# Loads, splits and small products at the head of a two-layer hybrid encoder kernel, in another order

## The chip, the core and the metric

The kernel runs on one core of a Trainium2 chip. The metric is the device time of one execution in microseconds (us), as the median of several runs; lower is better. The engines of the core are named PE (TensorE, the products), ACT (ScalarE), DVE (VectorE), POOL (GpSimd) and SP (SyncE, which here only issues transfers). ACT issues transfers too, on a queue of its own.

## What is computed

One inference step of a two-layer encoder trunk. 512 prompt tokens and 32 sample tokens, 544 in all, of width 1024, go through two layers. Only the beginning of a layer matters here: an RMS norm, a combined projection, and the low-rank gate of the gated linear attention (GLA).

```python
def rmsnorm(x, w):
    xf = x.astype(jnp.float32)
    y = xf * lax.rsqrt(jnp.mean(xf * xf, axis=-1, keepdims=True) + EPS)
    return (y * w.astype(jnp.float32)).astype(x.dtype)
...
    proj = (hn @ w_in_l).astype(jnp.float32)
...
    log_f = jax.nn.log_sigmoid(low @ w_a2_l.astype(jnp.float32) + b_a_l.astype(jnp.float32)) / GLA_TAU
```

`low` is 16 columns of `proj`. Retention, GLA, band attention, the output projection and a relu-squared MLP with 4096 hidden features follow in each layer, and a last RMS norm at the end.

## The kernel before

Activations stand with features on the partitions: `h` is 8 tiles (kc = 0 to 7) of 128 features by 544 tokens, held in SBUF throughout. Weights come as units of 128 by 1024 (512 KB): a unit is the 8 blocks of 128 by 128 that give 128 output features. A layer has 100 units: 28 of the input projection, 8 of the output projection, 64 of the MLP. Four buffers `raw[0..3]` take them in turn.

Products run in a fast float format of fewer bits, so each operand is split in two: `whi` (a rounded copy, made by ACT in `split`) and `wlo` (the rest, made by DVE in `rest`), and likewise `xhi` (`xhi_tile`, ACT, which also multiplies by the norm weights in the table `sm`) and `xlo` (`xlo_tile`, DVE). There are two buffers each of `whi` and `wlo`. A product block is three matmuls, whi by xhi, whi by xlo and wlo by xhi, over two halves of 272 tokens: 6 matmuls for each unit and kc, 48 for a unit (`products`).

The factor 1/rms is not put in ahead of the projection but afterwards, on the results. For it ACT squares the tiles (`squares`, into `nt[0]` and `nt[1]` in turn), DVE adds them up in `ssum` (`add_square`), and PE sums over the partitions with a matrix of ones (stage "rms", whole-array fp32 matmuls, 2 of them). DVE reads that out of PSUM into `ssum` (L908), makes `wlo` of unit 2, and then does a Newton step that ends in `rstd`. The low-rank product is stage "low": 16 small matmuls, each on a quarter of the array's columns, of `low_sb` (the low-rank weights, times the norm weights by `scale_low` on DVE) and `h`; it needs neither xhi nor xlo. Its result is multiplied by `rstd` and goes into stage "z".

What sets the order: each engine's program is written out by hand, in a function for each engine, and semaphores join them. PE does units 0 and 1 first; in layer 0 kc by kc, both units side by side, as the x tiles come in. Then, for each unit n from 2 on and each half of its tokens, it does the small stages listed in the table `PE_STEPS` under (n, half), and then the products. The tables `DVE_STEPS` and `ACT_STEPS` are copies of it with changes; both layers use them. Unit 2's accumulators share PSUM banks with the result of "rms", so `begin(2)` on PE waits for the semaphore `ms_ready`, which L908 raises, besides `w_lo`, which the third `rest` raises. (The program counts these over both layers.)

At the head of layer 0 the transfers are: on SP's queue x0, x1, x2, raw[1], x3 to x7, `low_sb`, `a2_sb`, raw[2], raw[3] and eight tables; on ACT's queue raw[0] and then the norm table `sm` (28 KB). Ahead of all products PE does 16 warm-up matmuls on ones.

Of the kernel before, what the change touches and what calls it, by code (L numbers as in the profile page):

```python
# [8 lines left out]
D = 1024  # L9
KC = D // P  # L10
# [15 lines left out]
UNITS = N_IN + N_OUT + GROUPS * N_MLP  # L26
PW = 2 * T
NEG = -1e30
YP = 2
WARM = 16  # L30
M0 = 4
# [5 lines left out]
ALU, ACT = mybir.AluOpType, mybir.ActivationFunctionType  # L37
# [6 lines left out]
GLA, RET = 0, 1  # L44
TOK = [(GLA, "v"), (GLA, "k"), (RET, "k"), (RET, "v")]
PE_STEPS = {
    (2, 0): [("rms",), ("low",)],
    (3, 0): [("z", 0)], (3, 1): [("z", 1)],
    (5, 0): [("diag", GLA)],
    (5, 1): [("level", 0)], (6, 0): [("level", 1)], (6, 1): [("level", 2)],  # L50
# [76 lines left out]
def f32(ap):  # L127
    return ap.bitcast(F32)
# [19 lines left out]
def hybrid_encoder(nc, x, wu, w_low, a2, small, bias, bias_s, st_ret, st_gla, ck, cv,  # L148
# [3 lines left out]
    with ctx:  # L152
# [95 lines left out]
        def sem(name):  # L248
            if name not in sems:
                sems[name] = ctx.enter_context(nc.semaphore(name))  # L250
            return sems[name]


        tables_in, sm_in, const_set, half_done, last_added = (
            sem(n) for n in ("tables_in", "sm_in", "const_set", "half_done", "last_added"))
        x_in = [sem(f"x_in{kc}") for kc in range(KC)]
        y_sums, y_mean, y_log, y_guess, y_col, y_wide, y_copied, y_scaled, y_dve, y_pool, y_out = (
            sem(n) for n in ("y_sums", "y_mean", "y_log", "y_guess", "y_col", "y_wide", "y_copied", "y_scaled",
# [21 lines left out]
        with nc.Block() as block:  # L280
            @block.sync
            def _(sp):
                for kc in range(KC):
                    sp.dma_start(h[:, kc, :], x[kc, :, :]).then_inc(x_in[kc], 16)
                    if kc == 2:
                        sp.dma_start(raw[1][:, :], wu[1, :, :]).then_inc(sems["w_in1"], 16)
                sp.dma_start(low_sb[:, :, :], w_low[0, :, :, :]).then_inc(sems["small_in"], 16)
                sp.dma_start(a2_sb[:, :], a2[0, :, :]).then_inc(sems["small_in"], 16)
                for n in range(2, RAW):
# [154 lines left out]
            def _(act):  # L444
# [4 lines left out]
                    ins.then_inc(sems["act_link"], 1)  # L449
                    act.wait_ge(sems["act_link"], links[0])  # L450

                act.dma_start(raw[0][:, :], wu[0, :, :]).then_inc(sems["w_in0"], 16)
                act.dma_start(sm[:, :], small).then_inc(sm_in, 16)

                for layer in range(L):
                    nth = counter(layer)
# [2 lines left out]
                    def split(n):  # L459

                        unit = layer * UNITS + n
                        if unit >= L * UNITS:
                            return
                        act.wait_ge(sems[f"w_in{n % RAW}"], 16 * (unit // RAW + 1))
                        if unit >= SPL:
                            act.wait_ge(sems["unit_done"], unit - SPL + 1)
                        nc.scalar.activation(whi[n % SPL][:, :], raw[n % RAW][:, :], ACT.Copy).then_inc(sems["w_hi"], 1)  # L467
# [5 lines left out]
                    def squares(kc, at_layer, cols=slice(0, T)):  # L473
                        if kc >= 2:
                            act.wait_ge(sems["ss_ready"], at_layer * KC + kc - 1)
                        nc.scalar.activation(nt[kc % 2][:, cols], h[:, kc, cols], ACT.Square).then_inc(sems["squared"], 1)

                    if layer == 0:
                        split(0)
                        act.wait_ge(sm_in, 16)  # L480
                        for kc in range(KC):
                            act.wait_ge(x_in[kc], 16)
                            xhi_tile(kc, 0)
                            if kc == 0:
                                split(1)
                            squares(kc, 0)
                    split(2)

# [260 lines left out]
            def _(dve):  # L749
# [7 lines left out]
                for layer in range(L):  # L757
# [12 lines left out]
                    def xlo_tile(kc, w, count):  # L770
                        dve.wait_ge(sems["x_hi"], nth("x_hi", count))
                        nc.vector.scalar_tensor_tensor(xlo[:, kc, :], h[:, kc, :], sm[:, w + kc:w + kc + 1],
                                                       f32(xhi[:, kc, :]), ALU.mult, ALU.subtract) \
                            .then_inc(sems["x_lo"], 1)
# [23 lines left out]

                    if layer == 0:
                        dve.wait_ge(sm_in, 16)  # L800
                        xlo_tile(0, 0, 1)
                        rest(0)
                        rest(1)
                        add_square(0, 0)
                        for kc in range(1, KC):
                            xlo_tile(kc, 0, kc + 1)
                            add_square(kc, 0)
                        scale_low(0)

                    def unit_out(n):  # L810

# [469 lines left out]
            def _(pe):  # L1281
# [6 lines left out]
                for layer in range(L):  # L1288
# [290 lines left out]

                    all_kc = tuple(range(KC))  # L1580
                    if layer == 0:
                        for kc in range(KC):
                            pe.wait_ge(sems["x_lo"], kc + 1)
                            for n in range(2):
                                if kc == 0:
                                    begin(n)
                                products(n, (xhi, xlo), (kc,), kc == 0, kc == KC - 1)
                    else:
                        pe.wait_ge(sems["x_lo"], nth("x_lo", KC - 1))
                        for n in range(2):  # L1590
                            begin(n)
                            products(n, (xhi, xlo), all_kc[:-1], last=False)
                        pe.wait_ge(sems["x_lo"], nth("x_lo", KC))
                        for n in range(2):
                            products(n, (xhi, xlo), all_kc[-1:], first=False)
# [187 lines left out]
```

## Time and profile before

| | |
|---|---|
| median of 3 runs | 1430.77 us (1430.03 to 1432.64) |
| the profiled execution's own time | 1430.05 us |
| its span, first to last instruction | 1428.2 us |
| PE busy | 1400.8 us (98%) |
| DVE busy | 773.3 us (54%) |
| ACT busy | 521.0 us (36%) |
| POOL busy | 147.2 us (10%) |
| mean granted TensorE clock | 0.995 of full speed |

Times in the profile count from the start of the span. Busy time of PE is not PE at its peak: matmuls are pipelined, each row's length includes filling and draining, and ends are modelled, so one row reaches over the start of the next. Spans of the other engines overlap in the same way by about a tenth of a microsecond. An idle time is put down to the semaphore event that came last.

### The profile page before, as it was taken

The numbers are of one execution on the slowest core, as the hardware profiler recorded it, in microseconds if no ns is written. First come the engines' busy times: TensorE is split into PE (matmuls) and PEld (weight loads), VectorE is DVE, ScalarE is ACT, GpSimd is POOL, SyncE is SP. The second block draws the span as 40 slices with busy tenths as digits, with TensorE's granted clock in tenths as the row PEclk, the third lists the DMA queues.
The fourth block names the chain that finished last, engine by engine and source line by source line (L and its number), as shares of the span: only waits on it lengthen the run. The fifth ranks groups of instructions, "written<-read, shape, count | busy, mean of one in ns | idle before, by whom it ended". The sixth has DMA issues, their size and how long they took to land.

```text
span 1428.2 us, 28637 instructions
## 1 busy us (share of the span) xinstructions
PE 1400.8 (98%) x12590; PEld 1359.4 (95%) x12590; DVE 773.3 (54%) x1224; ACT 521.0 (36%) x859; POOL 147.2 (10%) x107
## 2 busy tenths in 40 slices
PE   8999999999999999999999999999999999999996
PEld 8999889899999999999998999889999999999996
DVE  6797766744434334344767967765453443433433
ACT  5323556633213223123332236565332231321331
POOL 0200000031020110200202000001301102002012
PEclk9999999999999999999999999999999999999998
DMA  6123333222222222222221223422222222222211
GB/s 231 59 59 101 98 111 100 75 99 85 85 88 89 90 89 89 89 89 89 78 73 46 66 83 117 137 89 75 89 89 90 89 86 84 86 86 89 89 60 63
DMA packets 50635, 127.82 MB, mean 90 GB/s; under 512 B 8400, under 2 KB 17744, under 8 KB 50512
## 3 DMA queue, kind: packets, MB, share of 16 engines
q1 hardware_dynamic: 50224, 125.44, 27.0%
q8 instruction: 100, 1.64, 0.5%
q10 hardware_dynamic: 288, 0.55, 0.1%
q14 instruction: 23, 0.19, 0.0%
HBM read 118.77 MB, written 7.21 MB: 88 GB/s over the span
## 4 chain that ended last, share of the span: by engine, by line
PE 87%; DVE 5%; ACT 3%; issue 3%; POOL 1%; DMA 0%; POOLq 0%; SPq 0%; DVEq 0%; ACTq 0%
PE PS L1302 85%; ACT whi L467 1%; POOL h L435 1%; PE PS L1537 1%; ACT Pr L594 1%; PE PS L1416 1%; DVE Pr L1084 0%; DMA raw<-in_wu 0%; DVE F L889 0%; DVE gb L935 0%; DVE Pr L1096 0%; DVE sq L1203 0%; DVE wlo L767 0%; ACT xhi L470 0%; DVE O L877 0%
## 5 line engine op out<-in xcount | busy, mean ns | idle before, releaser
L1302 PE MATMUL PS<-xhi,whi 128*128 128x272 f32 x1920 | 562.9, 293 | 3.5 <-DVE wlo L767 2.6
L1302 PE MATMUL PS<-xhi,wlo 128*128 128x272 f32 x1920 | 555.2, 289 | 0.0
L1302 PE MATMUL PS<-xlo,whi 128*128 128x272 f32 x1920 | 552.7, 288 | 0.0
L767 DVE TENSOR_TENSOR wlo<-raw,whi 128x1024 fp32r<-128x1024 f32 x200 | 251.6, 1258 | 386.0 <-ACT whi L467 385.3
L467 ACT ACTIVATE whi<-raw 128x1024 fp32r<-128x1024 f32 x200 | 211.6, 1059 | 558.6 <-PE PS L1302 554.0
L1302 PEld LDWEIGHTS PS<-xhi,whi 128*128 128x128 f32 x1920 | 361.3, 188 | 15.5 <-issue 9.0
L1302 PE MATMUL PS<-zhi,wlo 128*128 128x272 f32 x1280 | 370.6, 290 | 0.0
L1302 PE MATMUL PS<-zhi,whi 128*128 128x272 f32 x1280 | 368.5, 288 | 0.4 <-DVE wlo L767 0.4
L1302 PE MATMUL PS<-zlo,whi 128*128 128x272 f32 x1280 | 368.5, 288 | 0.0
L1302 PEld LDWEIGHTS PS<-xlo,whi 128*128 128x128 f32 x1920 | 361.8, 188 | 0.2
L1302 PEld LDWEIGHTS PS<-xhi,wlo 128*128 128x128 f32 x1920 | 361.2, 188 | 0.0
L1302 PEld LDWEIGHTS PS<-zhi,whi 128*128 128x128 f32 x1280 | 241.0, 188 | 0.9 <-DVE wlo L767 0.9
L1302 PEld LDWEIGHTS PS<-zlo,whi 128*128 128x128 f32 x1280 | 241.1, 188 | 0.0
L1302 PEld LDWEIGHTS PS<-zhi,wlo 128*128 128x128 f32 x1280 | 240.8, 188 | 0.0
L435 POOL TENSOR_TENSOR h<-h,sq 128x544 f32<-128x544 f32 x62 | 89.3, 1441 | 653.1 <-DVE sq L1203 653.1
L662 ACT ACTIVATE zhi<-nt 128x544 fp32r<-128x544 f32 x64 | 42.2, 659 | 90.6 <-DVE nt L1192 90.6
L1195 DVE TENSOR_TENSOR zlo<-nt,zhi 128x544 fp32r<-128x544 f32 x64 | 50.0, 781 | 46.4 <-ACT zhi L662 46.4
L1203 DVE TENSOR_TENSOR sq<-PS,r 128x544 f32<-128x544 f32 x62 | 44.5, 718 | 20.6 <-PE PS L1302 14.5
L594 ACT ACTIVATE Pr<-Pr,mx 128x128 f32<-128x128 f32 (+1 forms) x64 | 35.2, 552 | 34.9 <-DVE mx L1089 34.9
L1192 DVE SCALAR_TENSOR_TENSOR nt<-PS,nt 128x544 f32<-128x544 f32 x64 | 46.0, 718 | 0.0
L426 POOL TENSOR_SCALAR ssum<-sq 128x544 f32<-128x544 f32 x2 | 2.4, 1183 | 416.9 <-ACT sq L651 416.9
L659 ACT ACTIVATE nt<-PS 128x544 f32<-128x544 f32 x64 | 38.8, 606 | 0.0
(226 smaller groups left out, 1083.0 us busy)
## 6 DMA issues: line engine op xcount, KB each, us to landing
raw<-in_wu SPq DMA_DIRECT2D x199, 512.0 KB, 3.5
Bh<-in_bias SPq DMA_DIRECT2D x16, 256.0 KB, 3.9
h<-in_x SPq DMA_DIRECT2D x8, 272.0 KB, 6.1
out_k_t<-att_k SPq DMA_DIRECT2D x8, 272.0 KB, 4.3
out_y_t<-y SPq DMA_DIRECT2D x8, 272.0 KB, 2.7
kct<-in_ck SPq DMA_DIRECT2D x8, 256.0 KB, 3.2
cvb<-in_cv SPq DMA_DIRECT2D x8, 256.0 KB, 5.0
out_v_p<-vtk SPq DMA_DIRECT2D x8, 256.0 KB, 2.2
```

The lines of the kernel that those rows point to most:

```text
L435: nc.gpsimd.tensor_tensor(h[:, m, :], h[:, m, :], sq[m % 2][:, :], ALU.add) \
L467: nc.scalar.activation(whi[n % SPL][:, :], raw[n % RAW][:, :], ACT.Copy).then_inc(sems["w_hi"], 1)
L594: ins = nc.scalar.activation(r, r, ACT.Exp, bias=mx[:, p, i:i + 1], accum_out=rs[:, p, i:i + 1])
L659: nc.scalar.activation(halves(r), PS[:, 2 * (n % 2):2 * (n % 2) + 2, 0:HT], ACT.Relu) \
L662: nc.scalar.activation(zhi[:, k, :], r[:, :], ACT.Copy).then_inc(sems["z_hi"], 1)
L767: nc.vector.tensor_tensor(wlo[n % SPL][:, :], raw[n % RAW][:, :], f32(whi[n % SPL][:, :]), ALU.subtract).then_inc(sems["w_lo"], 1)
L1192: nc.vector.scalar_tensor_tensor(halves(r), PS[:, 2 * (n % 2):2 * (n % 2) + 2, 0:HT], 0.0, halves(r), ALU.max, ALU.mult).then_inc(sems["un ...
L1195: nc.vector.tensor_tensor(zlo[:, k, :], r[:, :], f32(zhi[:, k, :]), ALU.subtract) \
L1203: nc.vector.tensor_tensor(halves(sq[m % 2]), PS[:, 2 * (n % 2):2 * (n % 2) + 2, 0:HT], halves(r2), ALU.mult).then_inc(sems["unit_read"], 1)
L1302: return nc.tensor.matmul(out, lhsT, rhs, start=start, stop=stop, skip_group_check=True)
L1416: nc.tensor.transpose(PS[:, M0 + g, i * P:(i + 1) * P], src[:, g * T + i * P:g * T + (i + 1) * P], ident[:, :])
L1537: last = nc.tensor.transpose(PS[:, M0 + b, c:c + P], Pr[p][:, P_OFF[i] + j * P:P_OFF[i] + (j + 1) * P], ident[:, :])
```

## The change

Four things are changed. The first unit's load is split in two halves of 512 columns (`HALF`), each with a semaphore; both stand at the head of ACT's queue and raw[1] follows them there, instead of standing on SP's queue. The norm table `sm` moves to the head of SP's queue. ACT and DVE split unit 0 in halves: the first half ahead of x0, the second behind x0, unit 1 behind x1, and only then come x2 to x7; the squares and their sums, which ran tile by tile among the splits, come after all of them. PE takes x0, x1 and x2 through unit 0 first (for kc below 4 only the first half of the unit is needed), then unit 1 catches up with these three, and from kc = 3 on both go side by side as before. In the table of steps, which both layers use, "low" stands ahead of "rms".

```diff
@@ -26,6 +26,7 @@
 UNITS = N_IN + N_OUT + GROUPS * N_MLP
 PW = 2 * T
 NEG = -1e30
+HALF = D // 2
 YP = 2
 WARM = 16
 M0 = 4
@@ -44,7 +45,7 @@
 GLA, RET = 0, 1
 TOK = [(GLA, "v"), (GLA, "k"), (RET, "k"), (RET, "v")]
 PE_STEPS = {
-    (2, 0): [("rms",), ("low",)],
+    (2, 0): [("low",), ("rms",)],
     (3, 0): [("z", 0)], (3, 1): [("z", 1)],
     (5, 0): [("diag", GLA)],
     (5, 1): [("level", 0)], (6, 0): [("level", 1)], (6, 1): [("level", 2)],
@@ -251,8 +252,8 @@
             return sems[name]
 
 
-        tables_in, sm_in, const_set, half_done, last_added = (
-            sem(n) for n in ("tables_in", "sm_in", "const_set", "half_done", "last_added"))
+        tables_in, sm_in, const_set, first_in, first_hi, first_lo, half_done, last_added = (
+            sem(n) for n in ("tables_in", "sm_in", "const_set", "first_in", "first_hi", "first_lo", "half_done", "last_added"))
         x_in = [sem(f"x_in{kc}") for kc in range(KC)]
         y_sums, y_mean, y_log, y_guess, y_col, y_wide, y_copied, y_scaled, y_dve, y_pool, y_out = (
             sem(n) for n in ("y_sums", "y_mean", "y_log", "y_guess", "y_col", "y_wide", "y_copied", "y_scaled",
@@ -280,10 +281,9 @@
         with nc.Block() as block:
             @block.sync
             def _(sp):
+                sp.dma_start(sm[:, :], small).then_inc(sm_in, 16)
                 for kc in range(KC):
                     sp.dma_start(h[:, kc, :], x[kc, :, :]).then_inc(x_in[kc], 16)
-                    if kc == 2:
-                        sp.dma_start(raw[1][:, :], wu[1, :, :]).then_inc(sems["w_in1"], 16)
                 sp.dma_start(low_sb[:, :, :], w_low[0, :, :, :]).then_inc(sems["small_in"], 16)
                 sp.dma_start(a2_sb[:, :], a2[0, :, :]).then_inc(sems["small_in"], 16)
                 for n in range(2, RAW):
@@ -449,8 +449,9 @@
                     ins.then_inc(sems["act_link"], 1)
                     act.wait_ge(sems["act_link"], links[0])
 
-                act.dma_start(raw[0][:, :], wu[0, :, :]).then_inc(sems["w_in0"], 16)
-                act.dma_start(sm[:, :], small).then_inc(sm_in, 16)
+                act.dma_start(raw[0][:, 0:HALF], wu[0, :, 0:HALF]).then_inc(first_in, 16)
+                act.dma_start(raw[0][:, HALF:D], wu[0, :, HALF:D]).then_inc(sems["w_in0"], 16)
+                act.dma_start(raw[1][:, :], wu[1, :, :]).then_inc(sems["w_in1"], 16)
 
                 for layer in range(L):
                     nth = counter(layer)
@@ -476,13 +477,18 @@
                         nc.scalar.activation(nt[kc % 2][:, cols], h[:, kc, cols], ACT.Square).then_inc(sems["squared"], 1)
 
                     if layer == 0:
-                        split(0)
+                        act.wait_ge(first_in, 16)
+                        nc.scalar.activation(whi[0][:, 0:HALF], raw[0][:, 0:HALF], ACT.Copy).then_inc(first_hi, 1)
                         act.wait_ge(sm_in, 16)
                         for kc in range(KC):
                             act.wait_ge(x_in[kc], 16)
                             xhi_tile(kc, 0)
                             if kc == 0:
+                                act.wait_ge(sems["w_in0"], 16)
+                                nc.scalar.activation(whi[0][:, HALF:D], raw[0][:, HALF:D], ACT.Copy).then_inc(sems["w_hi"], 1)
+                            if kc == 1:
                                 split(1)
+                        for kc in range(KC):
                             squares(kc, 0)
                     split(2)
 
@@ -798,14 +804,20 @@
 
                     if layer == 0:
                         dve.wait_ge(sm_in, 16)
-                        xlo_tile(0, 0, 1)
-                        rest(0)
-                        rest(1)
-                        add_square(0, 0)
-                        for kc in range(1, KC):
+                        dve.wait_ge(first_hi, 1)
+                        nc.vector.tensor_tensor(wlo[0][:, 0:HALF], raw[0][:, 0:HALF], f32(whi[0][:, 0:HALF]),
+                                                ALU.subtract).then_inc(first_lo, 1)
+                        for kc in range(KC):
                             xlo_tile(kc, 0, kc + 1)
+                            if kc == 0:
+                                dve.wait_ge(sems["w_hi"], 1)
+                                nc.vector.tensor_tensor(wlo[0][:, HALF:D], raw[0][:, HALF:D], f32(whi[0][:, HALF:D]),
+                                                        ALU.subtract).then_inc(sems["w_lo"], 1)
+                            if kc == 1:
+                                rest(1)
+                        scale_low(0)
+                        for kc in range(KC):
                             add_square(kc, 0)
-                        scale_low(0)
 
                     def unit_out(n):
 
@@ -1579,12 +1591,17 @@
 
                     all_kc = tuple(range(KC))
                     if layer == 0:
+                        pe.wait_ge(first_lo, 1)
                         for kc in range(KC):
                             pe.wait_ge(sems["x_lo"], kc + 1)
-                            for n in range(2):
-                                if kc == 0:
-                                    begin(n)
-                                products(n, (xhi, xlo), (kc,), kc == 0, kc == KC - 1)
+                            if kc == KC // 2:
+                                begin(0)
+                            products(0, (xhi, xlo), (kc,), kc == 0, kc == KC - 1)
+                            if kc == 2:
+                                begin(1)
+                                products(1, (xhi, xlo), (0, 1, 2), last=False)
+                            elif kc > 2:
+                                products(1, (xhi, xlo), (kc,), False, kc == KC - 1)
                     else:
                         pe.wait_ge(sems["x_lo"], nth("x_lo", KC - 1))
                         for n in range(2):
```

SP's queue, at the head of the program (numbers behind a name count buffers: `raw1_50` is raw[1], `h_57` is h, `sm_81` the norm table), one piece of the difference:

```order
-L284 DMA h_57<-in_x 128x544 x3
-L286 DMA raw1_50<-in_wu 128x1024
-L284 DMA h_57<-in_x 128x544 x5
+L284 DMA sm_81<-in_small 128x56
+L286 DMA h_57<-in_x 128x544 x8
 L287 DMA low_sb_79<-in_w_low 128x256
 L288 DMA a2_sb_80<-in_a2 128x256
```

The table stands ahead of all x tiles, and raw[1] is gone from between x2 and x3.

DVE at the head of layer 0, before (`raw_49` and `raw_50` are raw[0] and raw[1], `whi_53` and `wlo_55` belong to even units, `whi_54` and `wlo_56` to odd ones, `nt_67` and `nt_68` hold squares):

```order
L772 SCALAR_TENSOR_TENSOR xlo<-h,sm,xhi 128x544 [waits x_hi,sm_in]
L767 TENSOR_TENSOR wlo_55<-raw_49,whi_53 128x1024 [waits w_hi]
L767 TENSOR_TENSOR wlo_56<-raw_50,whi_54 128x1024 [waits w_hi]
L786 COPY ssum<-nt_67 128x544 [waits squared]
L772 SCALAR_TENSOR_TENSOR xlo<-h,sm,xhi 128x544 [waits x_hi]
L789 TENSOR_TENSOR ssum<-ssum,nt_68 128x544 [waits ss_ready,squared]
```

And now:

```order
L808 TENSOR_TENSOR wlo_55<-raw_49,whi_53 128x512 [waits first_hi,sm_in]
L778 SCALAR_TENSOR_TENSOR xlo<-h,sm,xhi 128x544 [waits x_hi]
L814 TENSOR_TENSOR wlo_55<-raw_49,whi_53 128x512 [waits w_hi]
L778 SCALAR_TENSOR_TENSOR xlo<-h,sm,xhi 128x544 [waits x_hi]
L773 TENSOR_TENSOR wlo_56<-raw_50,whi_54 128x1024 [waits w_hi]
L778 SCALAR_TENSOR_TENSOR xlo<-h,sm,xhi 128x544 [waits x_hi] x6
L801 TENSOR_TENSOR low_sb<-low_sb,sm 128x256 [waits small_in]
L792 COPY ssum<-nt_67 128x544 [waits squared]
```

xlo of x1 stands ahead of wlo of unit 1, and the sums come behind the last xlo. ACT's order moves in the same way: copy of the first half, xhi of x0, copy of the second half, xhi of x1, copy of unit 1, xhi of x2 to x7, and then the eight squares.

PE at the end of units 0 and 1 in layer 0, before:

```order
L1302 MATMUL PS<-xhi,wlo_56 128x272
L1302 MATMUL PS<-ssum,ones 128x272 [waits ss_ready]
L1302 MATMUL PS<-ssum,ones 128x272
L1302 MATMUL PS<-h,low_sb 32x272 [waits low_scaled]
L1302 MATMUL PS<-h,low_sb 32x272 x15
```

And now, with the first product of unit 2 behind it:

```order
L1314 MATMUL PS<-xhi,wlo_56 128x272
L1314 MATMUL PS<-h,low_sb 32x272 [waits low_scaled]
L1314 MATMUL PS<-h,low_sb 32x272 x15
L1314 MATMUL PS<-ssum,ones 128x272 [waits ss_ready]
L1314 MATMUL PS<-ssum,ones 128x272
L1314 MATMUL PS<-xhi,whi_53 128x272 [waits ms_ready,w_lo]
```

The two stages have changed places, here and in layer 1. On DVE the steps behind them keep their order: the read of the "rms" result (L920 now), wlo of unit 2, and the Newton step.

## Rows read from the trace of the kernel before

**Rows 1.** The page: shares of the chain that ended last, by engine.
```profile
PE 87%; DVE 5%; ACT 3%; issue 3%; POOL 1%; DMA 0%; POOLq 0%; SPq 0%; DVEq 0%; ACTq 0%
```

**Rows 2.** The chain in order of time, 0 to 45 us: start, length, what.
```profile
2.11 5.84 DMA raw<-in_wu
...
11.39 27.89 PE PS L1302 x224
```

**Rows 3.** Timeline, layer 0, PE and DVE: start, length, engine, line, operation, [idle before].
```profile
21.94 0.29 PE L1302 MATMUL PS<-xhi,wlo 128*128 128x272 f32 x1
22.07 1.08 PE L1302 MATMUL PS<-ssum,ones 128*128 128x272 f32 x4
23.08 2.04 PE L1302 MATMUL PS<-h,low_sb 128*32 128x272 f32 x32
25.10 0.39 PE L1302 MATMUL PS<-xhi,whi 128*128 128x272 f32 x1
...
23.18 0.72 DVE L908 TENSOR_SCALAR ssum<-PS 128x544 f32<-128x544 f32 x1 [2.90 <-PE PS L1302]
23.82 1.22 DVE L767 TENSOR_TENSOR wlo<-raw,whi 128x1024 fp32r<-128x1024 f32 x1
```

**Rows 4.** The same in layer 1, and the tile low_sb there (ns min/median/max, first and last start).
```profile
723.50 1.22 DVE L767 TENSOR_TENSOR wlo<-raw,whi 128x1024 fp32r<-128x1024 f32 x1
...
724.77 0.40 PE L1302 MATMUL PS<-xhi,whi 128*128 128x272 f32 x1
...
L1302 PE MATMUL PS<-h,low_sb x32: 392/393/417, 722.7 to 724.4; 128*32 128x272 f32 x32
```

**Rows 5.** Issues at 0.72, 0.75, 1.17, 2.11: size, us to landing; SP's first issues.
```profile
h<-in_x SPq DMA_DIRECT2D x1, 272.0 KB, 4.1
...
raw<-in_wu ACTq DMA_DIRECT2D x1, 512.0 KB, 4.3
...
h<-in_x SPq DMA_DIRECT2D x1, 272.0 KB, 4.7
...
raw<-in_wu SPq DMA_DIRECT2D x1, 512.0 KB, 5.8
...
0.72 1.34 SPq L284 DMA_DIRECT2D h<-in_x  x3
```

**Rows 6.** Stretches from 0: length, busy of each engine, clock, DMA share, mean GB/s.
```profile
0.00:4.30 4.30, 3.32 (x15) 3.33 (x16) 0.00 (x0) 1.28 (x1) 1.23 (x9) 1.00 0.54 190
...
0.00:6.40 6.40, 5.42 (x31) 5.42 (x32) 0.00 (x0) 2.56 (x3) 1.23 (x9) 1.00 0.71 255
0.00:7.10 7.10, 5.74 (x32) 5.55 (x32) 0.16 (x1) 2.98 (x3) 1.23 (x9) 1.00 0.74 269
```

**Rows 7.** Timeline of ACT and DVE at the head.
```profile
7.97 1.06 ACT L467 ACTIVATE whi<-raw 128x1024 fp32r<-128x1024 f32 x1 [1.15 <-DMA raw<-in_wu]
...
9.06 1.23 DVE L767 TENSOR_TENSOR wlo<-raw,whi 128x1024 fp32r<-128x1024 f32 x1 [0.20 <-ACT whi L467]
...
9.48 0.73 ACT L470 ACTIVATE xhi<-h,sm 128x544 fp32r<-128x544 f32 x1
...
10.55 0.78 DVE L772 SCALAR_TENSOR_TENSOR xlo<-h,sm,xhi 128x544 fp32r<-128x544 f32 x1
```

**Rows 8.** Timeline of PE around the first divided-array stage with a wait.
```profile
51.70 1.12 PE L1302 MATMUL PS<-QK 64*64 64x32 f32 x32 [1.08 <-DVE Ps L951]
52.75 0.39 PE L1302 MATMUL PS<-xhi,whi 128*128 128x272 f32 x1
```

**Rows 9.** PE waits at the head and the end; the granted clock is the third number from last.
```profile
9.00 0.36 PE L1302 MATMUL PS<-xhi,whi 128*128 128x272 f32 x1 [2.29 <-DVE wlo L767]
...
7.00:8.00 1.00, 0.00 (x0) 0.00 (x0) 1.00 (x2) 0.03 (x1) 0.00 (x0) 1.00 1.03 405
...
1410.46 1.58 PE L1651 MATMUL PS<-ones,ssum 128*128 128x1 f32 x10 [1.95 <-DVE ssum L1265]
...
1411.50:1412.00 0.50, 0.50 (x3) 0.46 (x3) 0.00 (x0) 0.00 (x0) 0.00 (x0) 0.50 0.12 33
```

## The prediction

> **What bounds the kernel now.** I read the page's chain first: 87% of the span's chain is TensorE (PE) and next to nothing is DMA [rows 1]. So a change at the head can only matter where PE has no work, and the places are few. The chain in order of time over the first 45 us says where: it comes from the SP queue through the landing of raw[1] at 7.95, ScalarE (ACT) and VectorE (DVE), and from 11.39 on it is PE alone for 27.9 us [rows 2]. Up to 11.39 PE has done 12 of the 96 products of units 0 and 1; the other 84 run back to back. So in the head the one number that counts is when the dense run starts: whatever moves 11.39 moves all that follows. The second view is PE beside DVE around the two small products ("rms" on ones and ssum, "low" on low_sb and h), 22 to 25 us and again 722 to 725 us in layer 1. There the reader should look at what ends just before the first product of unit 2: DVE's wlo of unit 2 ends at 25.04 and PE goes on at 25.10; in layer 1 at 724.72 and 724.77 [rows 3, 4]. The low product lies beside that DVE chain and hides it: rms is issued at 22.07, DVE reads it at 23.18, begins wlo of unit 2 at 23.82, and PE runs low from 23.08 to 25.12 [rows 3].
>
> **The head, step by step.** First the landings. Before, x0 and raw[0] run side by side on two queues and land at 4.8 and 5.05; x1 lands at 5.87, raw[1] at 7.95 [rows 5]. Cumulated bytes (rate times time) are 0.817 MB at 4.30, 1.632 at 6.40, 1.910 at 7.10 [rows 6]. x0 plus raw[0] are 0.803 MB, moved by 4.27; raw[0] lands 0.8 later. All up to raw[1] (norm table 0.029, two units 1.049, three x tiles 0.836) are 1.913 MB, moved by 7.1; it lands 0.85 later. That fits two queues that take turns transfer by transfer. In the changed kernel ACT's queue holds raw[0] in halves and then raw[1], SP's holds the table, x0, x1, ...: so x1 and raw[1] are a pair, with 0.029 + 1.049 + 0.557 = 1.635 MB moved by then, at 6.40; both land at about 7.25. raw[1] comes 0.7 earlier, x1 1.4 later. Transfers from x3 on have the same bytes ahead and stay.
>
> From 7.25: ACT makes xhi1 (0.73) and then whi of unit 1 (1.06); each operation starts some 0.1 before the end of the one ahead, as DVE's wlo at 23.82 does behind 23.18 + 0.72 [rows 3]: whi 7.9 to 8.95. DVE: wlo of unit 1 (1.23) 8.98 to 10.2, then xlo2 (0.78) 10.1 to 10.9 [rows 2, 7]. PE goes 0.06 after an xlo (10.55 + 0.78 = 11.33, PE at 11.39), so it is dense from 10.95. It has by then done 12 products (x0 and x1 of unit 0), 84 are left, as before. **Gain 0.44 us.** The halved first unit, the earlier table and the earlier first product (about 6.7, where the warm-up products end, instead of 9.00 [rows 9]) bring nothing by themselves: they only move PE's early 12 products about inside the idle time. The copies and subtractions of 512 columns cost at most 1.06 and 1.23 and lie in DMA waits.
>
> Bounds of that gain: if the queues share bytes equally instead, raw[1] waits until 2.10 MB are moved, 7.55 at the 0.40 MB/us between 6.40 and 7.10, and lands at 8.4; the same steps then give 11.45, no gain (a loss of 0.06). If x1 lands as early as before (5.87) and raw[1] at 7.25, whi starts at once and the run is dense from 10.3: a gain of 1.1. The rows fit the middle.
>
> **Squares summed last.** The eight xlo follow each other every 0.7, the last ends at 14.3; low_sb is scaled by 14.7; then a copy and seven adds that each wait for the one ahead, at the 0.72 of DVE's read of the same 544 columns [rows 3], 5.7 us with the gaps between them: the sum is ready by 20.5. PE ends units 0 and 1 at about 21.6. Hidden, with 1.1 us to spare, and 3 us with low ahead of it. whi of units 2 and 3 wait for PE anyway. Cost nothing.
>
> **Low ahead of rms**, which is in the table for both layers. The rms result is not only a sum: unit 2's products wait for DVE to read it (unit 2 writes the same banks), and DVE does wlo of unit 2 only behind that read. Moving low ahead of rms pushes this chain by the whole length of low, and takes away the work that hid it. Layer 0 with nothing else changed: the last product ahead ends at 21.94 + 0.29 = 22.23; at a change between whole and divided array the next product starts 0.07 before the modelled end (low 23.08 behind ones ending 23.15 [rows 3]; whole products 52.75 behind divided ones ending 52.82 [rows 8]). So low starts at 22.16, lasts 2.04, ones at 24.13; DVE reads 1.11 later at 25.24, wlo of unit 2 from 25.88 to 27.10, PE at 27.16 instead of 25.10: **2.06 us late**. Layer 1 is the same to 0.01 us [rows 4] and has no gain at its head: 2.06 again. Lower bound: ones starts one product spacing behind low's last start, 1.65 after its first [rows 4], a shift of 1.7. Upper: 2.1. I take 2.05, since both changes of form in the rows have the gap. Behind the start of unit 2 the order and all distances are as before (the Newton steps, rstd and wlo of unit 3 hang on the same chain), so nothing catches up or falls behind.
>
> The Trainium skill speaks to this switch: TensorEngine Tiling (Array Packing), Tiling Modes (Key Properties) says that a change of tiling mode drains the engine. The 0.07 us above are what this trace shows of it; with no drain the sum would use 1.7 instead of 2.05, and be 0.7 us smaller.
>
> **The sum.** -0.44 + 2 x 2.05 = +3.66 us. The profiled execution took 1430.05 us (span 1428.2 and 1.85 around it), so 1433.7; the median of the runs is 0.72 above the profiled one, so **1434.4 us**, 0.26% slower. About 0.2%, 2.9 us, is what a measurement of this kernel can tell from no change.
>
> **Rivals.**
> 1. The head gains the most it can. x1 lands at 5.87, and ones starts without a drain: -1.1 + 2 x 1.7 = +2.3, 1433.1 us, within 0.2%. For it: x1 did land that early. Against: it would have to pass half of raw[1] in the turn-taking that the landings show. It counts as no change from a sum of +2.9 down. Chance 0.2.
> 2. Not slower: the delay is taken up later. At 51.70 PE waits 1.08 us for DVE's masks (L951) [rows 8], in both layers. Were that DVE chain rooted in something that is not moved (a table's landing), up to 1.08 of each 2.05 would vanish: +3.66 - 2.16 = +1.5, 1432.3 us; all would vanish if other waits of that kind added up to 2, from which point it ends at or under the time before. Against: the chain view runs through PE up to 39 us and then through ACT's whi, released by PE [rows 2], so the wait moves with PE. Chance 0.11, of it 0.03 for faster.
> 3. The clock drops. Each layer now has PE idle for some 2 us ahead of unit 2 (ones ends at 25.2, products at 27.16). At the end of the kernel PE waits 1.95 us, runs ten narrow products, and the granted clock then falls from 1.00 to 0.50, that is from 2.4 to 1.2 GHz; between 6.72 and 9.00 it waits 2.3 us and the clock stays at 1.00 [rows 9]. If it fell for 2 to 4 us of dense products, each layer would lose 1 to 2 us more: about 1437. The Trainium skill (TensorE: Matmul & The Clock Gate, the part on the HAM clock gate) has the clock fall after an idle stretch; the trace has one case of each kind. Chance 0.07.
> 4. That the change does not do what it says is excluded for the swap by the instruction order; for the head it is the equal-bytes bound: 1434.9.
>
> **How the numbers follow.** Forecast 0.62 (nearly all of it beyond 0.2%: the sum with a gain of 0 to 0.7 and shifts of 1.85 to 2.1 is +3.0 to +4.2), rival 1 0.2, rival 2 0.11, rival 3 0.07. Slower: 0.66 (0.59 of the forecast, 0.07); no change: 0.31 (0.03, 0.2, 0.08); faster 0.03. The range takes the bounds +2.2 to +4.2, and 1 us each way for the runs' own spread (1430.03 to 1432.64): 1432.2 to 1436.0.
>
> **What would show it.** Right: PE dense from 10.6 to 11.2 with DVE's xlo2 as the releaser; whi of unit 1 released by ACT's own xhi1 or a landing near 7.2; PE idle 1.5 to 2.2 us between ones and the first product of unit 2 in both layers, released by wlo of unit 2; ones issued about 2 us after low; the last add of squares done 2 us or more ahead of ones. Wrong: a dense start before 10.4 (rival 1); a wait at the masks shorter than 1.08 (rival 2); a granted clock under 1.00 near 27 or 727 us (rival 3); or wlo of unit 2 done before ones is read, which would void the main term.

## The result and the profile after

| | before | after |
|---|---|---|
| median | 1430.44 us (1430.03 to 1432.64, 6 runs) | 1437.38 us (1434.19 to 1439.61, 6 runs) |
| ratio to before | | 1.0046, 95% interval 1.0032 to 1.0060 |
| span of the profiled execution | 1428.2 us | 1434.7 us |
| its mean granted clock | 0.995 | 0.992 |

Slower, as forecast, but by 6.9 us instead of 3.7 (against the 1430.77 known then, 6.6), and outside the range that ended at 1436.0. One run of the kernel `whole` below took 1998.38 us at a mean clock of 0.629 and is left out of its median.

The head first. The chain of the changed kernel in order of time (start, length, what), as [rows 2] of before:

```profile
1.64 5.51 DMA h<-in_x
...
7.17 0.75 ACT xhi L471
7.92 0.96 ACT whi L468
...
8.90 1.23 DVE wlo L773
10.13 0.71 DVE xlo L778
...
10.88 13.93 PE PS L1314 x120
```

x1 lands at 7.15, and the dense run starts at 10.88: 0.51 us earlier than the 11.39 of [rows 2], where 0.44 was forecast. Next the place where "low" and "rms" changed places; the timeline of PE and DVE, as [rows 3]:

```profile
21.64 2.04 PE L1314 MATMUL PS<-h,low_sb 128*32 128x272 f32 x32
23.61 1.18 PE L1314 MATMUL PS<-ssum,ones 128*128 128x272 f32 x4
26.75 0.39 PE L1314 MATMUL PS<-xhi,whi 128*128 128x272 f32 x1 [1.95 <-DVE wlo L773]
...
24.83 0.72 DVE L920 TENSOR_SCALAR ssum<-PS 128x544 f32<-128x544 f32 x1 [4.03 <-PE PS L1314]
25.48 1.22 DVE L773 TENSOR_TENSOR wlo<-raw,whi 128x1024 fp32r<-128x1024 f32 x1
```

PE sits idle for 1.95 us until DVE has made wlo of unit 2, as forecast; unit 2 starts 1.65 us later than in [rows 3], which with the head's 0.51 is 2.16 us for the order. In layer 1 the row is the same and comes at 730.19 instead of the 724.77 of [rows 4]:

```profile
730.19 0.41 PE L1314 MATMUL PS<-xhi,whi 128*128 128x272 f32 x1 [1.95 <-DVE wlo L773]
```

What the sum had not in it stands right behind. The stretches of one microsecond from 26 us on (busy time of PE, PE's loads, DVE, ACT, POOL, then granted clock, DMA share, GB/s), of layer 0 and of layer 1:

```profile
26.00:27.00 1.00, 0.26 (x2) 0.26 (x3) 0.69 (x1) 0.91 (x2) 0.00 (x0) 1.00 0.00 0
27.00:28.00 1.00, 1.00 (x7) 1.00 (x7) 0.93 (x2) 0.00 (x0) 0.00 (x0) 0.64 0.42 45
28.00:29.00 1.00, 1.00 (x7) 1.00 (x6) 0.96 (x2) 0.00 (x0) 0.00 (x0) 0.50 0.72 233
29.00:30.00 1.00, 1.00 (x6) 1.00 (x6) 0.93 (x3) 0.00 (x0) 0.00 (x0) 0.50 0.61 246
30.00:31.00 1.00, 1.00 (x7) 1.00 (x6) 1.00 (x2) 0.00 (x0) 0.00 (x0) 0.65 0.00 0
31.00:32.00 1.00, 1.00 (x10) 1.00 (x9) 1.00 (x3) 0.00 (x0) 0.00 (x0) 1.00 0.00 0
...
731.00:732.00 1.00, 1.00 (x7) 1.00 (x6) 0.94 (x2) 0.00 (x0) 0.00 (x0) 0.50 0.77 176
732.00:733.00 1.00, 1.00 (x6) 1.00 (x6) 0.96 (x2) 0.00 (x0) 0.00 (x0) 0.50 0.83 332
```

The granted clock falls from 2.4 to 1.2 GHz 0.5 us after unit 2 has begun in layer 0 (from 26.75 to 27.3) and 0.2 us after it in layer 1 (from 730.19 to 730.4), and comes back 3.4 us later. PE is busy all the time, with 6 or 7 products in a microsecond instead of 10: that is why busy time tells nothing here, and the clock column does. A product in these stretches:

```profile
27.10 0.29 PE L1314 MATMUL PS<-xhi,wlo 128*128 128x272 f32 x1
...
28.08 0.43 PE L1314 MATMUL PS<-xlo,whi 128*128 128x272 f32 x1
28.30 0.43 PE L1314 MATMUL PS<-xhi,wlo 128*128 128x272 f32 x1
```

Products start 0.226 us apart instead of 0.126. Added up in quarters of a microsecond, one minus the clock comes to 1.7 us for each of the two falls. The ledger of the profiled execution: unit 2 of layer 0 is 1.65 late; the dense run of layer 1 starts at 712.83 instead of 709.56, 3.27 late, so the fall kept 1.62; unit 2 of layer 1 is 5.42 late, 2.15 more for the order; the last product starts at 1415.10 instead of 1408.23, 6.87 late, 1.45 more from the second fall; and the small products on ones at the end take 1.28 us instead of 1.58, since there the clock fell later. That gives the 6.5 us between the spans. So each fall took 1.7 us of full clock, of which 1.62 and 1.45 arrived at the end.

### The profile page after: what moved, and what is told of

The parts are those of the page before. It is cut to its first block, busy times and chain, and to the rows that moved or that the text cites. A ratio compares the mean times of both kernels' runs of the same rounds, so it can differ in the third digit from the quotient of the medians.

```text
span 1434.7 us, 28641 instructions
## 1 busy us (share of the span) xinstructions
PE 1404.6 (98%) x12590; PEld 1363.0 (95%) x12590; DVE 774.3 (54%) x1225; ACT 521.8 (36%) x860; POOL 147.2 (10%) x107
## 4 chain that ended last, share of the span: by engine, by line
PE 87%; DVE 5%; ACT 3%; issue 3%; POOL 1%; DMA 0%; POOLq 0%; SPq 0%; DVEq 0%; ACTq 0%
PE PS L1314 85%; ACT whi L468 1%; POOL h L435 1%; PE PS L1549 1%; ACT Pr L600 1%; PE PS L1428 1%; DVE Pr L1096 0%; DVE wlo L773 0%; DMA h<-in_x 0%; DVE F L901 0%; DVE gb L947 0%; DVE Pr L1108 0%; ACT xhi L471 0%; DVE sq L1215 0%; DVE O L889 0%
```

## The experiments

Each kernel was run beside the kernel before on the same chip. The clock falls in some executions and not in others, at several places, so beside each median stands the lowest run. A trace shows one execution of a kernel only.

**rms_first**: the changed kernel without the swap.

```diff
-    (2, 0): [("low",), ("rms",)],
+    (2, 0): [("rms",), ("low",)],
```

> The changed kernel with the two small stages back in their old order (rms, then low), all else as changed. Theory (the loss is the order of the stages, and the clock that falls in the gap it opens; the head gives a small gain): the dense run of units 0 and 1 starts at 10.9, unit 2 at 24.6 instead of 26.75, no gap and granted clock 1.00 at both places, time 0.5 us under before, 1429.9. Rival (squares summed last, or the new landings, cost something as well): the ones product waits for the sum of squares, or the time is above before by 1 us or more.

1429.9 us (lowest 1428.5, 11 runs) against 1430.92, ratio 0.9993 (0.9984 to 1.0001). In its trace:

```profile
22.09 2.04 PE L1314 MATMUL PS<-h,low_sb 128*32 128x272 f32 x32
24.11 0.39 PE L1314 MATMUL PS<-xhi,whi 128*128 128x272 f32 x1
```

Dense from 10.43, unit 2 at 24.11 with no wait ahead of it, clock 1.00 at both places. The loss is gone with the swap, and the squares summed last cost nothing. A gain of the head isn't proven: 1 us lies between the medians, but the interval reaches past 1, and that the median is the expected 1429.9 is luck, since it was expected 0.5 below the kernel before and is 1.0 below.

**swap_only**: the kernel before with the swap alone.

```diff
-    (2, 0): [("rms",), ("low",)],
+    (2, 0): [("low",), ("rms",)],
```

> The kernel before with only the two small stages swapped (low, then rms). Theory: unit 2 starts 2.1 us later in each layer (27.2 instead of 25.10), and in the 2 us of idle PE ahead of it the clock falls to half for some 3 us in most executions: 4.3 us for the order and 1.6 us for each fall, 1437.9; executions without a fall near 1434.7. Rival (the clock falls owing to the changed head, which breaks up PE's early work): no falls, all executions near 1434.7.

1437.04 us (lowest 1435.05, 5 runs), ratio 1.0041 (1.0029 to 1.0054). Low at 23.55, ones at 25.53, and unit 2, in layer 0 and in layer 1, behind 1.95 us of idle PE as in the changed kernel:

```profile
28.66 0.39 PE L1302 MATMUL PS<-xhi,whi 128*128 128x272 f32 x1 [1.95 <-DVE wlo L767]
...
730.60 0.53 PE L1302 MATMUL PS<-xhi,whi 128*128 128x272 f32 x1 [1.95 <-DVE wlo L767]
```

In the profiled execution the clock falls behind the gap in layer 1 (0.50 from 730.7) and not behind the one in layer 0; it also falls once at the head, near 10.5, where the trace of before had none. Within the intervals the swap alone makes the whole loss, so the changed head is not what brings the falls.

**filler**: the changed kernel with PE kept busy in the gap.

```diff
-                            last.then_inc(sems["pe_low"], 1)
...
                             last.then_inc(sems["pe_rms"], 1)
                             give((2, 3), "ms_ready", 1)
+                            for _ in range(9):
+                                last = mm(PS[:, M0, 384:512], ones[:, :], ones[:, :])
+                            last.then_inc(sems["pe_low"], 1)
```

> The changed kernel with nine extra 128 by 128 products of ones by ones (their result is read by nobody) behind the rms product in each layer, in the gap ahead of unit 2, about 2 us of PE work. Theory (idle PE is what lets the clock fall): unit 2 still starts at 26.75, the clock stays at 1.00, the products of unit 2 keep their spacing of 0.126 us: 3.2 us less than the changed kernel in its usual executions, 1434.2, and the spread between executions shrinks. Rival (unit 2's slow products come from the loads that land beside them, not from the idle time): still slow, 1437.4.

The semaphore that lets the result of "low" be read is raised behind the extra products too, which doesn't move the start of unit 2.

1434.02 us (lowest 1433.32, 11 runs), ratio 1.0022 (1.0013 to 1.0031): 3.4 us under the changed kernel by the ratios (1.0046), 3.0 under swap_only beside it, and 1434.4 was the forecast without falls. The runs lie within 2.9 us, those of the changed kernel within 5.4. Timeline of PE in layer 0, and two stretches behind the start of unit 2:

```profile
25.58 1.18 PE L1314 MATMUL PS<-ssum,ones 128*128 128x272 f32 x4
26.60 2.17 PE L1314 MATMUL PS<-ones 128*128 128x128 f32 x18
28.71 0.39 PE L1314 MATMUL PS<-xhi,whi 128*128 128x272 f32 x1
...
30.00:31.00 1.00, 1.00 (x10) 1.00 (x10) 0.93 (x2) 0.00 (x0) 0.00 (x0) 1.00 0.86 295
...
732.00:733.00 1.00, 1.00 (x10) 1.00 (x10) 0.93 (x3) 0.00 (x0) 0.00 (x0) 1.00 0.60 221
```

Unit 2 starts 3.13 us behind ones, as in the changed kernel (3.14), so the order's price is untouched; only the idle time is gone, and with it both falls. The loads beside the products (0.86 of the DMA engines' time) don't slow them, which disposes of that rival, and the divided-array stage is still there ahead of ones, so it is not what brings the falls either. This execution, at 1436.16 us, has two falls elsewhere: one at 860.9, behind a wait of 1.13 us, and one at its late head:

```profile
10.75:11.00 0.25, 0.00 (x0) 0.00 (x0) 0.25 (x2) 0.25 (x2) 0.00 (x0) 1.00 1.05 374
11.00:11.25 0.25, 0.00 (x0) 0.00 (x0) 0.25 (x1) 0.25 (x1) 0.00 (x0) 0.52 1.16 421
...
11.60 0.59 PE L1314 MATMUL PS<-xhi,whi 128*128 128x272 f32 x1 [1.89 <-DVE xlo L778]
```

Here the clock falls while PE still waits, 0.6 us ahead of its next product.

**wlo_ahead**: wlo of unit 2 ahead of the read, on DVE, in the changed kernel.

```diff
+                            rest(2)
                             dve.wait_ge(sems["pe_rms"], nth("pe_rms", 1))
...
-                            rest(2)
```

> The changed kernel (low, then rms) with VectorE making wlo of unit 2 ahead of reading the rms result, so that only the read (0.72) stands between ones and unit 2. Theory: the gap shrinks from 1.95 to about 0.75 us, unit 2 starts at 25.55, the clock stays at 1.00: -0.5 + 1.0 + 1.0, 1431.9. Rival (the clock falls at this place for another reason than the idle time: the divided-array stage, or the loads that land there): falls remain, 1435.

1434.31 us (lowest 1431.65, 11 runs), ratio 1.0020 (1.0011 to 1.0029). The trace:

```profile
24.83 1.19 PE L1314 MATMUL PS<-ssum,ones 128*128 128x272 f32 x4
26.92 0.36 PE L1314 MATMUL PS<-xhi,whi 128*128 128x272 f32 x1 [0.91 <-DVE ssum L921]
...
33.04 1.08 PE L1314 MATMUL PS<-F,a_sb 128*128 128x272 f32 x4
34.19 0.39 PE L1314 MATMUL PS<-xhi,whi 128*128 128x272 f32 x1
```

The gap is 0.91 us and no fall stands behind it, in either layer. A new wait comes instead: from the small product on F to unit 3 it is 1.15 us where other kernels have 0.71, since the chain from the read over the Newton steps to wlo of unit 3 is now the later one. The lowest run agrees with the 1431.9 expected; the median doesn't, and in the profiled execution the clock falls at two other places (11.1, and 157.9 behind a wait of 1.14 us). Why falls elsewhere were more frequent here (the median lies 2.7 above the lowest run, against 1.2 in the kernel before) stays open.

**delay3** and **delay1**: wlo_ahead with the gap made longer by three DVE operations, or one.

```diff
                             dve.wait_ge(sems["pe_rms"], nth("pe_rms", 1))
+                            for _ in range(3):
+                                link(nc.vector.tensor_tensor(nt[1][:, :], ssum[:, :], ssum[:, :], ALU.mult))
```

> The kernel of wlo_ahead (low, then rms; wlo of unit 2 made ahead of the read) with three extra VectorE multiplications (0.76 us each, result read by nobody) ahead of the read of the rms result in each layer: a longer idle gap of PE ahead of unit 2, 3.1 us instead of 0.85, with the same work on PE. Theory (idle time of PE is what lets the clock fall, more surely the longer it is): unit 2 starts 2.3 us later in each layer, and the clock falls at both places in nearly every execution (3.4 us at half speed, 1.7 us lost each): 1431.7 without falls in wlo_ahead, plus 4.6, plus 3.4, plus other falls, about 1440.5. Rival (falls come by chance over the whole span and the gap does not matter): 2.7 us of falls as in wlo_ahead, 1439, and no fall at the two places in the trace.

> The kernel of wlo_ahead with one extra VectorE multiplication (0.76 us) ahead of the read in each layer: an idle gap of PE of 1.67 us ahead of unit 2, between wlo_ahead (0.91) and the changed kernel (1.95). Theory: unit 2 starts 0.76 us later in each layer than in wlo_ahead, and falls come at the two places in more executions than there and fewer than in delay3: lowest run 1433.2, median near 1436. Rival (no dependence on the gap's length between 0.9 and 3.2): lowest run 1433.2, and a median 2.7 above it as in wlo_ahead, 1435.9, so that only falls in the trace at unit 2 tell.

delay3: 1438.28 us (lowest 1436.14, 6 runs), ratio 1.0055 (1.0042 to 1.0068); the gaps are 3.19 and 3.18 us. The lowest run is 4.5 above that of wlo_ahead, as expected for 2 x 2.3; the median is 2.2 us short of what falls in nearly every execution would give. In the trace:

```profile
27.76 0.36 PE L1316 MATMUL PS<-xhi,whi 128*128 128x272 f32 x1 [3.19 <-DVE ssum L923]
...
29.00:30.00 1.00, 1.00 (x10) 1.00 (x10) 0.87 (x2) 0.00 (x0) 0.00 (x0) 1.00 0.00 0
...
731.22 0.36 PE L1316 MATMUL PS<-xhi,whi 128*128 128x272 f32 x1 [3.18 <-DVE ssum L923]
...
733.00:734.00 1.00, 1.00 (x7) 1.00 (x6) 0.97 (x2) 0.00 (x0) 0.00 (x0) 0.50 0.00 0
```

The same gap, once without a fall and once with it, within one execution. delay1: 1434.62 us (lowest 1433.41, 5 runs), ratio 1.0031 (1.0019 to 1.0043), gaps of 1.67 us, no fall at either place. All traces together, by the gap ahead of unit 2:

| gap ahead of unit 2 | kernels | places | falls |
|---|---|---|---|
| none or filled | before, rms_first, filler, later1, best, raw1_sp, whole, fill_all | 16 | 0 |
| 0.91 us | wlo_ahead | 2 | 0 |
| 1.67 us | delay1 | 2 | 0 |
| 1.95 us | after, swap_only | 4 | 3 |
| 3.2 us | delay3 | 2 | 1 |

At this place no fall came without idle time, and idle time is not enough. Whether a gap of 3.2 us brings more falls than one of 1.95 can't be read from six places, nor can a length below which none comes be read from four; that 3.2 us makes them near certain, as delay3 expected, is refuted. The other waits of these traces say the same: at the head the clock stays behind waits of 2.29 us (before) and 2.02 (best) and falls at ones of 2.23 (raw1_sp) and 1.89 (filler), and of the 48 waits of 1.06 to 1.14 us inside the two layers two are followed by a fall.

**raw1_sp** and **whole**: which part of the head gives the gain, from rms_first.

```diff
-                act.dma_start(raw[1][:, :], wu[1, :, :]).then_inc(sems["w_in1"], 16)
...
+                    if kc == 2:
+                        sp.dma_start(raw[1][:, :], wu[1, :, :]).then_inc(sems["w_in1"], 16)
```

> The kernel of rms_first with unit 1's transfer back on SyncE's queue behind x2, as before the change; the table stays at the head of that queue and unit 0 stays halved. Theory (two queues take turns transfer by transfer, so x1 and unit 1 land as a pair in the changed kernel): x1 lands near 5.9 and unit 1 near 8, the copy of unit 1 starts near 8.0 instead of 7.2 and the dense run at 11.2 instead of 10.4 to 10.9: 0.5 us slower than rms_first. Rival (the queues share bytes and unit 1's place does not matter): no difference in the dense start.

1430.7 us (lowest 1428.9, 11 runs), ratio 1.0001 (0.9992 to 1.0009), against the 0.9993 (0.9984 to 1.0001) of rms_first, so no difference in time is shown. ACT's timeline:

```profile
6.21 0.73 ACT L472 ACTIVATE xhi<-h,sm 128x544 fp32r<-128x544 f32 x1
8.13 1.06 ACT L469 ACTIVATE whi<-raw 128x1024 fp32r<-128x1024 f32 x1 [1.19 <-DMA raw<-in_wu]
```

Unit 1 lands at 8.1 and the dense run starts at 11.20, both as expected. But that doesn't settle what the place of unit 1 is worth: with the changed head the dense run starts at 10.43, 10.58, 10.66, 10.88, 11.34 and 11.60 in six traces, and 11.20 lies among them. Nor do x1 and unit 1 always land as a pair from two queues: 7.15 and 7.36 in the changed kernel, but about 7.05 and 8.5 in filler.

For whole, unit 0 is one transfer and one split again:

```diff
-                act.dma_start(raw[0][:, 0:HALF], wu[0, :, 0:HALF]).then_inc(first_in, 16)
-                act.dma_start(raw[0][:, HALF:D], wu[0, :, HALF:D]).then_inc(sems["w_in0"], 16)
+                act.dma_start(raw[0][:, :], wu[0, :, :]).then_inc(sems["w_in0"], 16)
```

> The kernel of rms_first with unit 0 loaded and split whole, not in halves. Theory (the halves only move TensorE's early twelve products inside idle time): the dense run still starts at 10.4 to 11.6 with the landing of x1 and unit 1, median within 0.2 us of rms_first, 1429.9. Rival (the halves carry the gain of the head): 0.5 us slower than rms_first.

1429.61 us, ratio 0.9993 (0.9984 to 1.0002), the same ratio as rms_first: the halves bring nothing that can be measured. Its trace is dense from 11.06. Which part of the head gives a gain, if any, stays open.

**later1** and **best**: unit 1 split behind x2; and with that wlo_ahead's edit (wlo of unit 2 ahead of the read), both from rms_first, in the old order of stages.

```diff
-                            if kc == 1:
+                            if kc == 2:
                                 split(1)
...
-                            if kc == 1:
+                            if kc == 2:
                                 rest(1)
```

> The kernel of rms_first (changed head, rms then low) with the copy and the rest of unit 1 made behind x2 instead of behind x1, on ScalarE and VectorE; TensorE's program is unchanged and needs unit 1 only behind unit 0's products with x2. Theory (the start of the dense run hangs on xlo of x2, which stands behind wlo of unit 1 on VectorE): x2 through unit 0 runs at 9.6 in what was idle time, unit 1 starts at 10.7 with 78 products left instead of 84: 0.8 us less than rms_first, 1429.1 as median. Rival (the landing of x2 at 7.9 and ScalarE's copies hold it up as much): within 0.2 us of rms_first.

> The kernel of later1 with wlo of unit 2 made ahead of the read of the rms result on VectorE. Theory: low hides the read, so unit 2 starts when low is done (some 0.3 us earlier in each layer), and the chain over the read to unit 3 keeps 0.3 us to spare: 0.6 us less than later1, 1428.5 as median. Rival (the read is pushed back behind wlo of unit 2, and with it the Newton steps and unit 3): no gain over later1, or a loss of 0.3.

later1: 1429.31 us (lowest 1427.99), ratio 0.9992 (0.9983 to 1.0000). best: 1429.57 us (lowest 1428.01), ratio 0.9992 (0.9983 to 1.0001). later1 takes x2 at 9.65, but unit 1 only at 11.04, and ones starts at 21.01 against 21.08 in rms_first: six products moved forward, and unit 1 as much later. In best the place of unit 2 is

```profile
22.11 1.18 PE L1314 MATMUL PS<-ssum,ones 128*128 128x272 f32 x4
23.23 2.04 PE L1314 MATMUL PS<-h,low_sb 128*32 128x272 f32 x32
...
22.65 1.23 DVE L773 TENSOR_TENSOR wlo<-raw,whi 128x1024 fp32r<-128x1024 f32 x1 [0.59 <-ACT whi L468]
```

with unit 2 at 25.20, 3.09 behind ones (2.98 in layer 1; 3.03 before): wlo is done at 23.88 and gains nothing, because low itself ends at 25.27. So in [rows 3] low and wlo end together, and neither hides an idle time that could be had: 0.3 us a layer was expected, 0.04 and 0.05 came (unit 2 is 3.13 and 3.03 behind ones in later1). Neither kernel is proven faster than before, or than rms_first, where 0.8 and 1.4 us were expected.

**fill_all**: later1 with extra products of ones in PE's other short waits (`busy` issues that many 128 by 128 products of ones by ones).

```diff
+                            if kc < 2:
+                                busy(PS[:, M0, 384:512], 2 + 2 * kc)
...
+                            if piece == 0 and l == 0:
+                                busy(PS[:, bank(5) + 1, 384:512], 4)
...
                             take(0, 1, 2)
+                            busy(PS[:, M0, 0:P], 4)
```

> The kernel of later1 with extra products of ones by ones (read by nobody) in TensorE's short waits: two behind x0's and four behind x1's products at the head, four ahead of the first level stage and four ahead of each of the two transposes of the normalised outputs, in both layers. Theory (the clock falls behind waits of about 1 us too, in a part of the executions, and costs 1.7 us each time): no fall in the trace before the last stretch, the runs close up at their lower end, median 0.7 us under later1, 1428.6. Rival (falls have nothing to do with these waits, or the fillers delay what follows them): same median as later1 or above.

1430.64 us (lowest 1429.87, 11 runs), where 1428.6 was expected, ratio 1.0003 (0.9995 to 1.0012), beside a kernel before at 1430.05. No fall in its trace ahead of the last stretch, and a spread of 1.75 us from lowest to highest against 3.4 in later1; but the lowest run is 1.9 us above that of later1, so the fillers cost more than the falls they spare. Which of them costs it was not taken apart.

## Why the prediction was wrong

The terms that the sum had in it held, each against its row, one of them by luck. **Landings**: x1 and unit 1 as a pair near 7.25, measured 7.15 and 7.36 in this trace; but in other executions of the same transfers x1 was taken at 6.72 (rms_first) or only at 8.43 (best), and in filler unit 1 came 1.5 us behind x1, so the turn-taking that the prediction read from one trace isn't shown as a rule. **Gain of the head**: 0.44 forecast, 0.51 found, and that is luck: with the same head the dense run started anywhere from 10.43 to 11.60, a gain of 0.96 to a loss of 0.21 against the one trace of before. **Squares last**: the last add ended at 20.81, 2.8 us ahead of ones, cost nothing. **The order**: 2.05 a layer forecast, 2.16 and 2.15 found. The tenth missing is in the ones product, which takes 1.18 us instead of the 1.08 of [rows 3], 1.22 to DVE's read instead of 1.11. Why is open: it does so behind the divided array in every trace, but in layer 0 of later1 and best behind the whole array too. Idle PE of 1.95 us against "some 2 us", with wlo of unit 2 as the releaser.

As to the switch between divided and whole array: ones starts 1.97 us after low, which lasts 2.04; the prediction's lower bound, without a drain, was 1.7. The Trainium skill (TensorEngine Tiling (Array Packing), Tiling Modes, Key Properties) has it drain the engine, and the trace agrees. The sum without a drain, 0.7 us smaller, would have been further off.

The step that failed is the clock, **rival 3**: the sum has no term for it, and holds that behind the start of unit 2 "nothing catches up or falls behind". The prediction had the mechanism, its place and its price (a loss of 1 to 2 us in each layer, about 1437; measured 1.7 for each fall, two in the profiled execution, and a median of 1437.4), but gave it a chance of 0.07 and ended the range at 1436.0, below that price. (The lower end, +2.2 less 1, would be 1432.0 and not 1432.2; nothing hangs on it.) The reason given was one case of each kind in [rows 9]: at the head PE waits 2.29 us and the clock stays, at the end it waits 1.95 and the clock falls. One profiled execution was read as if the clock did the same each time. It does not: at the head the clock fell in 4 of the 13 traces (swap_only, wlo_ahead, filler, raw1_sp), and in layer 0 and layer 1 of one kernel the same gap went both ways. Without its falls the sum comes out: the profiled execution took 1436.62, less the 1.62 and 1.45 of the ledger 1433.55, where the prediction had 1433.7 for that execution; and the lowest run of the changed kernel, 1434.19, has the highest mean clock of the six, 0.995. How many falls the others had isn't shown: the highest, 1439.61, is 5.4 above the lowest, three falls by their size, yet its mean clock is 0.992, as in the profiled execution with two. A warning lay in the runs of before: 1430.03 to 1432.64 is a spread of 2.6 us, one fall and a half, and the prediction took it for noise of 1 us each way. Of the 27 runs of before beside rms_first the eight lowest have a mean clock of 0.995, the six above 1432 one of 0.991 to 0.993.

With the expected cost of the falls in the sum (in traces with a gap of 1.95 us, 3 of 4 places, times 1.7, times two layers: 2.6 us) it would have come to 1437.0; that is hindsight, since the 3 of 4 were counted afterwards. The Trainium skill (TensorE: Matmul & The Clock Gate, Part 1) has the clock fall after an idle stretch; three of the four gaps of 1.95 us here agree, the fourth doesn't.

Shown: the swap makes the loss (rms_first, swap_only); some 3 of the 7 us come through the idle time and not through the chain (filler: 3.4 by the ratios, 1 to 6 by their intervals). Not settled: why a gap of the same length brings a fall in one place and not in the other, whether the chance grows with the length, and whether gaps of 1.7 us and less at this place ever bring one; elsewhere two of 48 waits of about 1.1 us did.

## What to carry to other kernels

When two stages change places, look at what the later one was hiding: here a product that nobody waited for soon stood behind one whose result opened a chain of a read and a split, and moving it ahead exposed the whole chain, in both layers, since the table serves both. Price an idle gap that a change opens on TensorE at its length plus the chance of a fall of the clock, and take that chance from the clocks of many executions, not from one trace. A gap that can't be closed can be filled with products that nobody reads, if they cost less than the falls, as in filler and not in fill_all.

## What the runs showed of the hardware

The granted clock stayed at 0.50 for 3.4 us in each of the ten falls ahead of the end of the kernel, 1.70 to 1.71 us of full clock each, wherever it came. It fell at no fixed distance from the idle time: in filler at 11.0, 0.6 us before PE had work again (11.60); in the changed kernel 0.5 and 0.2 us after unit 2 had begun; in delay3 at 732.8, 1.6 us after it had (731.22). So the slow products need not stand next to the gap. Transfers that are issued alike land at other times in each execution: with the same transfers ahead x1 was there at 6.72 in one trace and at 8.43 in another, and unit 1 came 0.2 us behind it in one and 1.5 us behind it in a third.
